# The adaLN product of a two-layer encoder step on four column groups of the TensorE array

## The reference

```python
def modulate(x, c, g, w_ada, b_ada):
    mod = jnp.dot(jax.nn.silu(c), w_ada) + b_ada
    shift, scale, gate = jnp.split(mod, 3, axis=-1)
    h = rmsnorm(x, g) * (1 + scale[:, None]) + shift[:, None]
    return h, gate[:, None]
```

## Time and profile before

| | us |
|---|---|
| median of 3 runs | 2710.42 |
| lowest and highest | 2710.17, 2716.11 |
| span of the profiled execution | 2720.3 |
| PE busy | 2572.7 (95%) |
| PEld busy | 2180.8 (80%) |
| DVE busy | 994.4 (37%) |
| ACT busy | 818.7 (30%) |
| POOL busy | 868.0 (32%) |
| mean granted TensorE clock | 0.975 |

### The profile page before, as it was taken

The page is one execution under the profiler, slowest core; times in us unless marked ns, Lnnn a source line. Parts: engine busy times, 40 slices in busy tenths (PEclk is TensorE's granted clock), DMA queues, the critical chain, the costliest instruction groups (busy, mean ns, idle before and its releaser), DMA issues.

```text
span 2720.3 us, 52410 instructions
## 1 busy us (share of the span) xinstructions
PE 2572.7 (95%) x16711; PEld 2180.8 (80%) x16711; DVE 994.4 (37%) x1779; ACT 818.7 (30%) x1546; POOL 868.0 (32%) x651
## 2 busy tenths in 40 slices
PE   7999999999999999879999999999999999996997
PEld 2227879899999989779922388898999999896997
DVE  2241346776111234431103423487731122344113
ACT  0012334444333333322200133344433333333221
POOL 5012224334333333334300232343343333342341
PEclk8999999999999999989999999999999999998999
DMA  8983222223333323234478622232233333222443
GB/s 264 346 287 104 55 57 74 73 71 88 90 90 97 80 75 82 59 110 133 151 239 276 214 72 54 63 81 69 74 98 88 93 85 80 76 68 73 136 125 131
DMA packets 410102, 311.75 MB, mean 115 GB/s; under 512 B 21304, under 2 KB 347840, under 8 KB 408712
## 3 DMA queue, kind: packets, MB, share of 16 engines
q1 hardware_dynamic: 382296, 283.35, 35.8%
q10 hardware_dynamic: 27632, 26.21, 3.1%
HBM read 280.81 MB, written 30.92 MB: 115 GB/s over the span
## 4 chain that ended last, share of the span: by engine, by line
issue 56%; PE 20%; POOL 19%; POOLq 2%; DMA 1%; DVE 0%; SPq 0%; DVEq 0%; ACT 0%; ACTq 0%
POOL w_lo L458 18%; PE misc L513 6%; PE proj L572 4%; PE proj L566 4%; PE proj L568 4%; POOL act_lo L451 1%; POOLq L443 1%; POOLq L441 1%; POOLq L465 1%; POOLq L457 0%; PE misc L521 0%; DMA out_y_prompt<-work 0%; PE misc L489 0%; DVE work L1159 0%; DMA raw<-in_w_in 0%
## 5 line engine op out<-in xcount | busy, mean ns | idle before, releaser
L566 PE MATMUL proj<-act_hi,w_hi 128*128 128x288 f32 (+1 forms) x4672 | 1336.6, 301 | 29.2 <-DVE act_lo L1156 20.1
L568 PE MATMUL proj<-act_lo,w_hi 128*128 128x288 f32 (+1 forms) x4672 | 1312.1, 296 | 0.0
L458 POOL TENSOR_TENSOR w_lo<-raw,w_hi 128x512 fp32r<-128x512 f32 (+1 forms) x584 | 778.4, 1336 | 1432.6 <-ACT w_hi L866 1432.4
L572 PE MATMUL proj<-act_hi,w_lo 128*128 128x288 f32 (+1 forms) x4672 | 1004.1, 296 | 0.0
L566 PEld LDWEIGHTS proj<-act_hi,w_hi 128*128 128x128 f32 (+1 forms) x4672 | 883.1, 189 | 58.8 <-issue 48.0
L568 PEld LDWEIGHTS proj<-act_lo,w_hi 128*128 128x128 f32 (+1 forms) x4672 | 883.6, 189 | 3.4
L572 PEld LDWEIGHTS proj<-act_hi,w_lo 128*128 128x128 f32 (+1 forms) x4672 | 752.3, 188 | 0.0
L866 ACT ACTIVATE w_hi<-raw 128x512 fp32r<-128x512 f32 (+1 forms) x584 | 365.6, 629 | 1186.5 <-PE proj L572 1141.9
L513 PE MATMUL misc<-work,sc 128*2 128x512 f32 x768 | 344.8, 607 | 18.7 <-DMA work<-in_w_ada 11.5
L513 PEld LDWEIGHTS misc<-work,sc 128*2 128x2 f32 x768 | 64.2, 86 | 278.6 <-issue 278.3
L451 POOL TENSOR_TENSOR act_lo<-xy,act_hi 128x576 fp32r<-128x576 f32 x32 | 50.2, 1582 | 352.7 <-ACT act_hi L873 296.2
(11 more groups left out here) (169 smaller groups left out, 1695.0 us busy)
## 6 DMA issues: line engine op xcount, KB each, us to landing
raw<-in_w_in SPq DMA_DIRECT2D x448, 256.0 KB, 2.9
work<-in_w_ada SPq DMA_DIRECT2D x96, 1024.0 KB, 5.2
raw<-in_w_out SPq DMA_DIRECT2D x128, 256.0 KB, 2.8
x_keep<-xy ACTq DMA_DIRECT2D x32, 288.0 KB, 2.5
lb<-x_keep SPq DMA_DIRECT2D x24, 288.0 KB, 3.3
x_keep<-xy ACTq DMA_DIRECT2D x4, 1152.0 KB, 11.6
out_y_prompt<-work SPq DMA_DIRECT2D x4, 1024.0 KB, 3.9
qi_raw<-x_keep SPq DMA_DIRECT2D x8, 288.0 KB, 3.8
```

Of the source, the lines that this page charges most:

```text
L458: pool.tensor_tensor(w_lo[:, c, :, 0:width], raw[:, c, :, 0:width], w_hi[:, c, :, 0:width].bitcast(F32), ALU.subtract)\
L566: pe.matmul(dst, w_hi[:, c, kk, 0:width], act_hi[:, k, cols], start=(k == 0), stop=False)
L568: pe.matmul(dst, w_hi[:, c, kk, 0:width], act_lo[:, k, cols], start=False, stop=False)
L572: m = pe.matmul(proj[b][0:width, half, 0:HALF], w_lo[:, c, kk, 0:width], act_hi[:, k, cols], start=False, stop=(k == KT - 1))
```

## The change

The four matmuls of a transfer go to four groups of 32 columns of the array, one k tile in each. Group kk writes two partitions, 32 kk and 32 kk + 1, of the same bank, and sums over the four transfers alone (start at s = 0, stop at s = 3). A block still has 16 matmuls, of the same shapes. The copy takes all 128 partitions of the bank, and the turn multiplies by `sel`, 128 x 2, whose ones stand at rows 0, 32, 64, 96 (first column) and one below each (second column), so that it adds the four partial sums while it makes columns. `sel` is built once by DVE from the identity, and both banks are set to zero once, before the first layer; PE waits for this ahead of the first block.

```diff
+        sel = sb("sel", [P, 2])
...
-        ada_row = [sqb[0:2, n, 0:AB] for n in (1, 2)]
+        ada_row = [sqb[:, n, 0:AB] for n in (1, 2)]
...
             pe.wait_ge(c_ready, 1)
+            pe.wait_ge(sel_ready, 1)
...
                         for kk in range(KC):
-                            k = s * KC + kk
-                            m = pe.matmul(s_ps[n][0:2, :], sc[:, k, :], ada_w[:, s, kk, :],
-                                          start=(k == 0), stop=(k == KT - 1))
+                            m = pe.matmul(s_ps[n][32 * kk:32 * kk + 2, :], sc[:, s * KC + kk, :],
+                                          ada_w[:, s, kk, :], start=(s == 0), stop=(s == 3),
+                                          tile_position=(0, 32 * kk), skip_group_check=True)
                         m.then_inc(ada_used, 1)
...
                         m = pe.matmul(t_ps[:, bass.ds(j * 8 + 2 * i, 2)], ada_row[n][:, i * P:(i + 1) * P],
-                                      ident[0:2, 0:2], start=True, stop=True)
+                                      sel[:, :], start=True, stop=True)
...
+            dve.drain()
+            for a in (0, 1):
+                dve.memset(s_ps[a], 0.0)
+            dve.tensor_tensor(sel[:, :], ident[:, 0:2], ident[:, 32:34], ALU.add)
+            for a in (64, 96):
+                dve.drain()
+                dve.tensor_tensor(sel[:, :], sel[:, :], ident[:, a:a + 2], ALU.add)
+            dve.drain().then_inc(sel_ready, 1)
             dve.wait_ge(const_in, CONSTS * 16)
...
-                    dve.tensor_copy(ada_row[n], s_ps[n][0:2, :]).then_inc(ada_read, 1)
+                    dve.tensor_copy(ada_row[n], s_ps[n]).then_inc(ada_read, 1)
```

More of the change, by code:

```diff
@@ L184, in build @@
         c_ready = sem("c_ready")
+        sel_ready = sem("sel_ready")
         vec_in = sem("vec_in")
```

## The result

| | before | after |
|---|---|---|
| median, us | 2713.27 (4 runs) | 2637.15 (4 runs) |
| lowest and highest | 2710.17, 2720.56 | 2634.94, 2642.81 |
| span of the profiled execution | 2720.3 | 2641.0 |
| mean granted TensorE clock | 0.975 | 0.926 |

The ratio of after to before is 0.9717, with a 95% interval of 0.9698 to 0.9736. The change makes the kernel about 76 us faster. Forecast were 2611 us, in a range from 2595 to 2665: the direction, the mechanism and the bound that takes over were right, and the gain came out at about three quarters of what was summed. The profiled execution of the kernel after is the slowest of its four (2642.81 us); its span is 1.8 us shorter than the time of that run.

What follows compares the result with a forecast made beforehand. PE was taken as the bound, with DMA following and becoming the bound after the change. Gains of 31.3 + 47 + 22 = 100 us took the span from 2720.3 to 2620, so a median of 2611 us, range 2595 to 2665.

Steps and rivals of the forecast that it cites:

- The third sign: Before the change, SyncE's queue, which reloads used slots, waits 149.5 us on L513 in layer 1; read as PE being the bound.
- SyncE's wait on L513 nearly gone: Announced for the profile after: the wait of SyncE's queue on the product, 149.5 us in layer 1 before, would nearly vanish.
- About 3 (5 us a block): Overlap factor taken for the product's matmuls: 10 us a block with turns at 1.2 GHz; block 11 about 5 us.
- rivals 2 and 3: In L513: no overlap, 2711 us, chance 0.09; or changing column group makes records cost their whole 0.592 us, 2833 us, 0.09.
- Rival 1: Product overlaps only partly, factor near 1.2, or 2 at half clock; PE stays the bound, 2660 up to 2700 us; chance 0.08.
- the 390 taken: DMA rate in GB/s assumed for the product once DMA leads, near two rows with full queues: 10.7 us a block.
- the cautious 325: Low-end DMA rate in GB/s, from 284 at a q1 busy share of 0.874 scaled to full; would give 2655 us.
- layer 0, turn of block 7: Product's first part: 44.7 MB at 390 GB/s puts this turn at 142.7 instead of 174.03, 31.3 us gained.
- layer 1, start to turn of block 7: Product's first part: 33.55 MB from 1369 at 390 GB/s puts the turn at 1456 instead of 1503.13, 47 us gained.
- The start of layer 1: First slot free about 2 us after PE starts at 1364.89, 2 us more to the first byte: data flow from 1369.
- The tail: After block 7's turn, VectorE's modulation, about 30 us, becomes the bound; only block 11 gains, 10.5 + 11.5 = 22 us.
- From span to median: Forecast span 2620 turned into median 2611 us by subtracting 9.9, the profiled span 2720.3 against the median 2710.42 before.

## Why the prediction was right, and where its sum was off

**The bound before** was PE. Halved transfers left the kernel before almost unchanged, and the rows had said it: PE busy through the whole stretch, and 284 GB/s where more was possible. The third sign that I used, SyncE waiting for L513, says nothing of it: the same wait is 102.4 us in the changed kernel, where DMA is the bound. The conclusion was right, but this step to it was not, and "SyncE's wait on L513 nearly gone" was the one announced sign that failed.

**The factor.** Read from two row groups, it held for column groups: four at once give four. (L597 itself shows a little under two: 1.35 us less 0.16 of run-out is 1.2, against 2.1.) That column groups would behave like row groups was a guess that no row backed. "About 3 (5 us a block)" was cautious; at the full clock a block would take at most 4 x 1.04 us, at the half clock twice 3.69, as 16 records took at 150.57, less the run-out. Neither matters under a block's transfer time, but block 11 stands outside that cover.

**The rivals.** No overlap and exposed hiding (rivals 2 and 3) are out: 8 records in 1.04 us. The weight loads of four groups on the same rows do run under matmuls: the 768 loads of 87 ns fit into 14.9 us of busy time, and at 150.57 all eight loads of a transfer start within 0.02 us, seven of them after the first matmul record, of 1.01 us, has begun. The rule of the Trainium skill, "TensorE: Matmul & The Clock Gate", Part 3 (The mechanism), that a weight load overlaps running matmuls only when the row group differs, does not hold for this kernel; the trace decides. Rival 1 (PE stays the bound) is excluded by PE's waits for slots. DMA's rate was 380 to 387 GB/s, near the 390 taken and not the cautious 325: the two rows with several slots outstanding were the right guide, and scaling a rate by the busy share was not. The other terms held: VectorE copied block 6 at 127.8, 11 us before block 8 began at 138.8, and the zeroing and `sel` took 2.7 us (0.9 to 2.3 were allowed) while PE waited for weights until 30.02, so they cost nothing.

**The sum**, by the milestones of the two profiled executions (turn of block 7, start of the projection L569, start of the next layer's product):

| step | predicted | measured | off |
|---|---|---|---|
| layer 0, turn of block 7 | 142.7 | 148.77 | 6.1 |
| layer 0, from there to the projection | 40.6 | 43.6 | 3.0 |
| projection 0 to product 1 | as before, 1139.8 | 1141.0 | 1.2 |
| layer 1, start to turn of block 7 | 91.1 | 98.95 | 7.9 |
| layer 1, from there to the projection | 41.2 | 43.5 | 2.3 |

Together 20.5 us, against 100 summed and 79.3 found in the spans. A second profile of the changed kernel, from its later run, has 148.1, 42.4, 1140.1, 98.6 and 43.6, so the misses in both first parts and in layer 1's tail repeat within 0.7 us. The terms that were too small are of three kinds.

*Bytes and rate, first part.* In layer 0 the rate was 380 GB/s and not 390, which is 3.0 us over 44.7 MB. DMA had moved 45.55 MB when block 8 was in, 0.85 MB of it for later slots: 2.2 us. The turn followed the last slot's landing by 1.8 us, not 1.1, for the clock was low: 0.7. That makes 5.9 of the 6.1 us. The bias windows are the main reason for the lower rate, as moving them (and x_keep with them) showed.

*The start of layer 1.* The sum let data flow 4.1 us after PE's first matmul, 2 of them for PE to use up the first slot. But PE ran at the lower clock there and stood still in the middle of the slot:

```profile
1333.35 1.87 PE L515 MATMUL misc<-work,sc 128*2 128x512 f32 x3 [3.16 <-issue]
1336.69 1.14 PE L515 MATMUL misc<-work,sc 128*2 128x512 f32 x4 [1.47 <-issue]
```

SyncE issued the first reload at 1338.86, 5.5 us after 1333.35 and not 2, and data flow from about 1340.5: 3.1 us. From there to the last slot's landing at 1430.4 it took 90 us and not 86: 4.0. About 2 of them are 0.75 MB that moved ahead for later slots, the rest is the rate:

```profile
DMA packets 17240, 34.30 MB, mean 377 GB/s; under 512 B 512, under 2 KB 512, under 8 KB 17237
```

(1339.5 to 1430.4). The last slot and the clock make 0.8 more, as in layer 0. The trace of before already had the pause, where it cost nothing because PE was the bound. The earlier trace rows stop just short of it:

```profile
1368.19 14.48 PE L513 MATMUL misc<-work,sc 128*2 128x512 f32 x29 [0.82 <-issue]
```

There too PE starts at the lower clock and stops once more, and SyncE issued the first reload only at 1372.65, 7.8 us after the first matmul. All four slots were full and nothing moved; "after about 2 us" should have been read from this.

*The tail.* VectorE's 30 us came out as forecast and set the end of the product. Block 11 took 6.4 us and not 5, as it ran at the lower clock for most of its length (0.50 from 183.85 to 189): 1.4 us in each layer. The rest, 1.6 us in layer 0, lies ahead of it: the turns of blocks 7 and 9 took 1.87 and 1.84 us instead of about 1. The copy's lateness as the bound of the tail was forecast; that moving it would give 12 to 16 us was not borne out by the times.

*From span to median.* I subtracted the 9.9 us by which the profiled span of before lay above the median of then. For the changed kernel this difference is 3.9 us. That is 6.0 us of the miss and no mechanism at all, only which execution was profiled: 2610 + 20.7 + 6.0 = 2637. Two profiles of the changed kernel have spans of 2641.0 and 2632.5.

## What to carry to other kernels

When a stage is bound by a thin matmul (here two columns of 128), count what its transfers need per block before costing the faster matmul; the gain ends there, and here a factor of two bought the same. Take DMA's limit from stretches with several transfers outstanding, add every byte that shares the stage, and look for the first moment at which all buffers are full. A queue that waits for a buffer to come free does so whichever side is the bound: look at whether the consumer waits for the landing. Then follow each engine that hides behind the old bound: here a copy queued behind 30 us of VectorE's work, 2.8 us of waiting before and 11.7 after, was the next thing to move, though its wait did not arrive whole in the time.

## What the runs showed of the hardware

- Four f32 matmuls of two columns in four column groups run in the time of one: eight records in 1.04 us at the full clock, against 3.6 us in one group. Each reads its own 128 x 512 operand. Two groups took 1.89 us for the same eight records.
- Groups overlap further than to the next matmul: with the four matmuls of a transfer in one group, a block still fell from 13.83 to 9.82 us when the next transfers had landed, and records started out of the program's order, three ahead of the one that ended the first transfer.
- The granted clock fell to 0.50 for most of the product with four groups (PE busy 11.53 of 14 us) and stayed at 1.00 with two (busy 15.75 of 20), though the busy shares are alike. At the full clock four groups left rests of 1.67 us and two left 0.8; the fall came in such a rest. With four groups at 0.50 and with two at 1.00 a slot takes the same 1.89 us.
- Sixteen DMA engines with up to four transfers of 1 MB outstanding, in pieces of 2 KB, moved a steady 387 GB/s. Taking a DRAM to DRAM transfer of 2.1 MB from beside them raised the mean from 380 to 392 GB/s and brought the end of that stage 11 us forward.
- SyncE's queue waited for PE to free a slot for about as large a share of the time when PE was the bound (93.6 of 115 us) as when DMA was (64.3 of 85).
